# Sum transfers issued ahead of the weight sums, and down-projection weights loaded in single blocks

## The reference

```python
up = jnp.einsum('btd,df->btf', x, w_up)                 # 1024 -> 2 * 2816
hp = jnp.concatenate([conv_prefix, up], axis=1)
hc = conv_b + sum(conv_w[i] * hp[:, i:i + T] for i in range(CONV_WIDTH))   # width 3, per channel
g, u = hc[..., :D_FF], hc[..., D_FF:]
y = jnp.einsum('btf,fd->btd', jax.nn.gelu(g, approximate=False) * u, w_down)
x = layer_norm(DEEPNORM_ALPHA * x + y, ln2_g, ln2_b)
```

## Time and profile before

| What | Value |
| --- | --- |
| median of 3 runs | 2557.95 us (2546.45 to 2564.44) |
| the profiled execution | 2561.84 us, of which span 2560.1 us |
| PE busy | 2222.9 us (87%), 13868 matmuls |
| DVE, ACT, POOL busy | 63%, 41%, 36% |
| SP's DMA queue (q1) | 261.69 MB, 32.7% of the 16 DMA engines' span |
| POOL's DMA queue (q0) | 74.98 MB, 17.7% |

### The profile page before, as it was taken

The page is one execution under the profiler, slowest core; times in us unless marked ns, Lnnn a source line. Parts: engine busy times, 40 slices in busy tenths (PEclk is TensorE's granted clock), DMA queues, the critical chain, the costliest instruction groups (busy, mean ns, idle before and its releaser), DMA issues.

```text
span 2560.1 us, 35253 instructions
## 1 busy us (share of the span) xinstructions
PE 2222.9 (87%) x13868; PEld 1989.6 (78%) x13868; DVE 1609.4 (63%) x2064; ACT 1044.0 (41%) x1867; POOL 930.9 (36%) x554
## 2 busy tenths in 40 slices
PE   7999998888788887599899999989889888876996
PEld 7987678888788885478788866789888887854875
DVE  1569668666665665355836686777566665662557
ACT  3227565333333334245522375553333333341543
POOL 1134255454444542301221334555444444332112
PEclk9999999999899998799999999999989999987998
DMA  6221462444444448969651215614434444599695
GB/s 167 67 52 36 126 187 77 113 106 105 106 111 104 103 102 261 273 168 221 165 153 43 56 32 161 195 63 112 106 94 119 103 116 100 127 274 263 160 212 155
DMA packets 257468, 338.92 MB, mean 132 GB/s; under 512 B 39184, under 2 KB 157712, under 8 KB 257232
## 3 DMA queue, kind: packets, MB, share of 16 engines
q1 hardware_dynamic: 222424, 261.69, 32.7%
q0 software_dynamic: 34880, 74.98, 17.7%
HBM read 217.65 MB, written 98.03 MB: 123 GB/s over the span
## 4 chain that ended last, share of the span: by engine, by line
PE 31%; DVE 17%; POOL 16%; DMA 16%; issue 10%; ACT 8%; SPq 1%; ACTq 0%; POOLq 0%; DVEq 0%
DMA e_scr<-hg 11%; PE ps L2718 10%; PE ps L2306 8%; DMA araw<-a_scr 5%; POOL wblk L973 4%; POOL wblk L969 3%; PE ps L2565 3%; POOL bl L961 3%; DVE hg L1878 2%; DVE hg L1875 2%; POOL wblk L980 2%; POOL wblk L977 2%; ACT hg L1311 2%; PE ps L2626 2%; ACT bh L1274 1%
## 5 line engine op out<-in xcount | busy, mean ns | idle before, releaser
L2626 PE MATMUL ps<-bt,bh 128*128 128x272 f32 (+1 forms) x3520 | 629.7, 303 | 152.4 <-ACT gu L1283 137.2
L2626 PEld LDWEIGHTS ps<-bt,bh 128*128 128x128 f32 x3520 | 535.6, 202 | 162.3 <-ACT gu L1283 145.9
L2626 PE MATMUL ps<-bt,bl 128*128 128x272 f32 (+1 forms) x1760 | 384.4, 300 | 0.0
L1274 ACT ACTIVATE bh<-wblk 128x512 fp32r<-128x512 f32 x308 | 181.5, 622 | 490.5 <-POOL wblk L973 283.9
L2718 PE MATMUL ps<-dh,ah 128*128 128x512 f32 x616 | 257.9, 419 | 100.7 <-DVE al L1918 98.4
L961 POOL TENSOR_TENSOR bl<-wblk,bh 128x512 fp32r<-128x512 f32 x98 | 160.3, 1638 | 427.4 <-ACT bh L1274 427.4
L2626 PEld LDWEIGHTS ps<-bt,bl 128*128 128x128 f32 x1760 | 295.2, 201 | 0.0
L2718 PE MATMUL ps<-dl,ah 128*128 128x512 f32 x616 | 252.0, 409 | 0.0
L2718 PE MATMUL ps<-dh,al 128*128 128x512 f32 x616 | 251.3, 408 | 0.0
L2626 PE MATMUL ps<-ba,bh 128*128 128x272 f32 (+2 forms) x1408 | 235.6, 289 | 16.3 <-DVE gu L1864 14.6
L1841 DVE TENSOR_TENSOR bl<-wblk,bh 128x512 fp32r<-128x512 f32 x210 | 165.0, 819 | 124.0 <-ACT bh L1274 124.0
(11 more groups left out here) (260 smaller groups left out, 4444.4 us busy)
## 6 DMA issues: line engine op xcount, KB each, us to landing
wblk<-in_w_up SPq DMA_DIRECT2D x88, 512.0 KB, 5.3
a_scr<-hg SPq DMA_DIRECT2D x44, 552.0 KB, 3.2
e_scr<-hg POOLq DMA_DIRECT2D x44, 512.0 KB, 7.0
araw<-a_scr SPq DMA_DIRECT2D x66, 256.0 KB, 8.4
araw<-e_scr SPq DMA_DIRECT2D x66, 256.0 KB, 6.1
w<-in_w_down POOLq DMA_DIRECT2D x16, 1024.0 KB, 16.6
wrow<-in_w_out SPq DMA_DIRECT2D x48, 256.0 KB, 5.1
wrow<-in_w_out SPq DMA_DIRECT2D x24, 512.0 KB, 4.5
```

The lines of the kernel that those rows point to most:

```text
L1274: act.activation(bh[b][:], block_of(f, b), ACT.Copy).then_inc(S["u_hi"], 1)
L2626: e = nc.tensor.matmul(up_half(f, b, n), lhs, rhs[:, c:HW_] if n else rhs[:, 0:c], start=(k == 0 and m == 0), stop=(k == HK - 1 and m == 2))
```

## The change

In the up loop POOL issues `act_add(k, 0)` and `act_add(k, 1)` behind the low half of B_12 and ahead of the four weight sums, instead of after them; `act_add(k, 2)` stands before B_S3's sum instead of after it.

In the down stage w21, w22 and w12 are loaded in 33 transfers of 256 KB, one per step of SP's list from s = 4 to s = 36, in order of use, on two semaphores; block `i` waits for block `i - 2` to have landed. The rows for the residual come back one per step (s = 5 to 8 and s = 20 to 23). POOL's first weight sum moves behind R_TOP, and ACT's negated copies move by up to four steps. SP's wait for `adds1` moves from s = 14 to s = 20, and the second pair of gains from s = 26 to s = 38.

```diff
+            def down_block(l, i):
+                n, k = divmod(i, KP)
+                tile, c = ((w21, 0), (w22, HT), (w12, HT))[n]
+                if i >= 2:
+                    sp.wait_ge(S[f"wb{i % 2}"], wb_count(l, i - 2))
+                src = w_down[l].rearrange("(k two p) n -> two p k n", two=2, p=P)[1]
+                sp.dma_start(tile[:, k, :], src[:, k, c:c + HT]).then_inc(S[f"wb{i % 2}"], 16)
...
-                    elif s in (5, 7):
+                    elif 5 <= s < 9:
+                        if s == 6:
+                            sample_raw(l, 2)
                         z_back(l, s - 5)
-                        z_back(l, s - 4)
-                    elif s == 6:
-                        sample_raw(l, 2)
-                        down_block(l, "w21", 0, 0, 6)
-                    elif s == 8:
-                        down_block(l, "w21", 1, 6, KP)
...
-                    elif s == 12:
-                        down_block(l, "w12", 2, 8, KP)
-                    elif s in (14, 16):
-                        if s == 14:
-                            sp.wait_ge(S["adds1"], 16 * KP * (l + 1))
-                        z_back(l, s // 2 - 3 + (s - 14) // 2)
-                        z_back(l, s // 2 - 2 + (s - 14) // 2)
-                    elif s == 15:
-                        sp.wait_ge(S["sm_lo"], 4 * (l + 1))
-                        down_block(l, "w12", 0, 0, 4)
-                    elif s == 17:
-                        down_block(l, "w22", 0, 0, KP)
...
+                    elif 20 <= s < 24:
+                        if s == 20:
+                            sp.wait_ge(S["adds1"], 16 * KP * (l + 1))
+                        z_back(l, s - 16)
+                    elif s == 26:
+                        sp.wait_ge(S["sm_lo"], 4 * (l + 1))
                         sp.wait_ge(S["neg"], neg_t(l, T_1, 0) + 1)
-                        down_block(l, "w12", 1, 4, 8)
-                    elif s == 26:
+                    elif s == 38:
...
+                    if s < 4 + 3 * KP:
+                        down_block(l, s - 4)
                     act_block(l, s)
...
                     lo_up(l, f, B_12)
+                    if f >= 3:
+                        act_add(l, (f - 3) // 2, 1 - f % 2)
                     for b in SUMS[:3]:
                         sum_up(l, f, b)
-                    sum_up(l, f, B_S3)
                     if f >= 5 and f % 2:
                         act_add(l, (f - 5) // 2, 2)
-                    if f >= 3 and f % 2:
-                        act_add(l, (f - 3) // 2, 0)
-                    elif f >= 4:
-                        act_add(l, (f - 4) // 2, 1)
+                    sum_up(l, f, B_S3)
...
-                weight_add(l, T_1, 0)
                 for t in range(4):
                     residual(l, t)
                 act_add(l, KP - 1, 1)
                 residual_add(l, R_TOP)
+                weight_add(l, T_1, 0)
+                act_add(l, KP - 1, 2)
+                residual_add(l, R_P1)
                 weight_add(l, T_1, 1)
-                act_add(l, KP - 1, 2)
                 weight_add(l, T_1, 2)
-                residual_add(l, R_P1)
```

More of the change, by code:

```diff
@@ L462, in zb_count, with wb_count @@
             return 16 * (4 * l + 4) if t == NB else 16 * (2 * l + 2 + len(range(t // 2, NTOK, XS)))
+        def wb_count(l, i):
+            return 16 * (l * len(range(i % 2, 3 * KP, 2)) + i // 2 + 1)
         def rows_bank(i):
@@ L623, in up_cols, with first_blocks @@
                         .then_inc(S[f"wu_landed{f % 2}"], 16)
[L625 to L630, removed]
+            def first_blocks(l, n, k0, k1):
+                src = w_down[l].rearrange("(k two p) n -> two p k n", two=2, p=P)[0][:, k0:k1, 0:HT]
+                at_ = w12[:, 4 + k0:4 + k1, :] if k0 < 4 else w11[:, k0:k1, :]
+                sp.dma_start(at_, src).then_inc(S[f"wc_landed{n}"], 16)
+            def down_block(l, i):
[5 more added lines that the diff above has]
+                sp.dma_start(tile[:, k, :], src[:, k, c:c + HT]).then_inc(S[f"wb{i % 2}"], 16)
             def act_block(l, s):
@@ L848, in body @@
                         sp.wait_ge(S["u_lov"], lo_n(l, FT - 2, B_S4))
-                        down_block(l, "w11", 0, 0, 2)
-                        down_block(l, "w11", 1, 2, 4)
+                        first_blocks(l, 0, 0, 2)
+                        first_blocks(l, 1, 2, 4)
                         sample_raw(l, 0)
@@ L861, in body @@
                 sp.wait_ge(S["u_p"], 7 * (l + 1) * FT)
-                down_block(l, "w11", 2, 4, 7)
-                down_block(l, "w11", 3, 7, KP)
+                first_blocks(l, 2, 4, 7)
+                first_blocks(l, 3, 7, KP)
                 for s in range(4, NST):
@@ L881, in body @@
                         neg_out(l, KP - 1, 1)
-                    elif s == 12:
-                        down_block(l, "w12", 2, 8, KP)
-                    elif s in (14, 16):
-                        if s == 14:
-                            sp.wait_ge(S["adds1"], 16 * KP * (l + 1))
-                        z_back(l, s // 2 - 3 + (s - 14) // 2)
-                        z_back(l, s // 2 - 2 + (s - 14) // 2)
-                    elif s == 15:
-                        sp.wait_ge(S["sm_lo"], 4 * (l + 1))
-                        down_block(l, "w12", 0, 0, 4)
-                    elif s == 17:
-                        down_block(l, "w22", 0, 0, KP)
                     elif s == 18:
                         conv_rows(l, NRB - 1)
-                    elif s == 21:
+                    elif 20 <= s < 24:
[4 more added lines that the diff above has]
+                        sp.wait_ge(S["sm_lo"], 4 * (l + 1))
                         sp.wait_ge(S["neg"], neg_t(l, T_1, 0) + 1)
-                        down_block(l, "w12", 1, 4, 8)
-                    elif s == 26:
+                    elif s == 38:
                         sp.wait_ge(S["e_out"], 16 * KP * (l + 1))
@@ L1336, in weight_neg @@
                 elif which == T_3:
-                    act.wait_ge(S["w12"], 48 * (l + 1))
+                    for i in (2 * KP + k1 - 1, 2 * KP + k1 - 2):
+                        act.wait_ge(S[f"wb{i % 2}"], wb_count(l, i))
                     out, src = w12, w12[:, k0:k1, :]
@@ L1354, in down_hi @@
                     act.wait_ge(S[f"wc_landed{slot}"], wc_count(l, OUTU + slot))
[L1355 to L1358, removed]
+                elif p in (P_2, P_3):
+                    i = k + (KP if p == P_3 else 0)
+                    act.wait_ge(S[f"wb{i % 2}"], wb_count(l, i))
                 else:
@@ L1594, in body @@
                         scaled_gains(l)
-                        weight_neg(l, T_1, 0)
                     elif s == 6:
@@ L1599, in body @@
                         sample_hi(l, 3)
-                        weight_neg(l, T_1, 1)
+                        weight_neg(l, T_1, 0)
                     elif s == 10:
                         first_out(l)
-                    elif s == 11:
-                        weight_neg(l, T_1, 2)
+                    elif s in (12, 15):
+                        weight_neg(l, T_1, s // 3 - 3)
                     elif s in (26, 30, 33):
                         weight_neg(l, T_2, (26, 30, 33).index(s))
[L1607 to L1610, removed]
+                    elif s in (36, 38, 40):
+                        weight_neg(l, T_3, s // 2 - 18)
+                    elif s in (41, 42, 44):
+                        weight_neg(l, T_4, (41, 42, 44).index(s))
                     elif 58 <= s < 63:
```

## The result

The changed kernel takes **2332.09 us** (median of 4 runs, 2325.63 to 2335.54) against 2557.91 us for the kernel before on the same chip: a ratio of **0.9119**, 95% interval 0.908 to 0.9157. The forecast was 2342 us.

What follows compares the result with a forecast made beforehand. Bound: in the up stage a late landing of POOL's adding transfer, in P_1 and P_2 the DMA engines. 2561.8 (profiled) - 182 - 34 = 2346, which stands 3.9 above the median, so 2342 us; range 2290 to 2420.

Steps and rivals of the forecast that it cites:

- what bounds the kernel now: Up stage: PE held by ACT's tap_gate, which waits for POOL's adding transfer to land; P_1 and P_2: DMA engines.
- Rival E: Up stage: the landing was not the last to come, tap_gate has another reason to wait; no chance of its own.
- Step 1: Up loop, adds ahead of the sums: turn 26.4 to 21.6 us, issue priced 0.1 to 0.4; 91 us a layer, 182 in both.
- Rival A: Up loop: the issue can't start beside DVE's tap and is paid in full, 22.6 us a turn, 2380 us; chance 0.14.
- rival D: Up loop: the add's wait for e_out, ahead of the sums, makes it slower than before, 2632 us; chance 0.04.
- rival C: Up loop: the add's landing in its new place takes 16 instead of 7.0 to 9.83 us, 2426 us; chance 0.05.
- Step 2: Down stage, weights in single blocks: P_1 and P_2 win 23 us, P_3 loses 6; net 17 a layer, 34 in both.
- rival B: Down stage gives nothing, as SP waits for blocks, and P_3 pays: +8 us a layer, 2392 us; chance 0.14.
- w12, 2.9 MB, 9 us: Down stage: w12's load leaves the stretch before s = 22, taking 9 us of DMA time with it.
- term for R_BOT and its rows: Down stage: R_BOT, 12.6 us, and about half of the rows fetched at s = 20 to 23, 3 us, leave P_1 and P_2.
- Not won: the four scalings: Down stage: rz_top's four scalings stay back to back; they hold DVE's split of a tile for 11.87 us.
- Step 3: Down stage, the rest: SP's issues of 33 blocks are hidden and later landings have slack; cost 0.

Runs made afterwards that it cites:

- e1: The kernel before with only the up loop's new order, the adds ahead of the sums; down stage as before: 2356.20 us, ratio 0.9211.
- e3: The changed kernel with one further 64 KB transfer issued by POOL right behind the add in each turn: 2347.19 us, ratio 0.9177.
- e4: The changed kernel with three further 64 KB transfers issued by POOL right behind the add in each turn: 2388.82 us, ratio 0.9335.
- e9: The changed kernel with act_add(k, 0) and act_add(k, 1) moved from ahead of to behind the first three weight sums: 2368.57 us, ratio 0.9273.
- e2: The changed kernel with the up loop's order put back, so only the down stage's part of the change: 2530.67 us, ratio 0.9888.
- e6: The changed kernel with four semaphores for blocks, so SP waits for block i - 4 instead of i - 2: 2329.79 us, ratio 0.9119.
- e10: The changed kernel with the bias adds R_TOP and R_BOT cut to 64 of 1024 columns: 2309.73 us, ratio 0.9046.
- e11: The changed kernel with w12 loaded in three transfers at s = 12, 15 and 21, as before the change: 2329.68 us, ratio 0.9124.
- e8: The changed kernel with the last four residual rows and the adds1 wait back at s = 14 and 16: 2344.24 us, ratio 0.9174.
- e7: The changed kernel with six large weight transfers in the same order instead of single blocks, no wait for blocks: 2335.29 us, ratio 0.9135.
- e5: The changed kernel with POOL waiting, ahead of each residual scaling, for its own scaling before: 2329.68 us, ratio 0.9112.

## Why the prediction was right

**The bound (step "what bounds the kernel now")** was read rightly: the landing that led the chain was the last thing that `tap_gate` waited for, and it is gone. Rival E falls with that.

**Step 1, the adds ahead of the sums: right in mechanism, 17 us too small.** 91 us a layer were forecast; it was 101.3 and 97.7 by `tap_gate`, 202 us in both by e1. The term that was mis-sized is the price of the issue, "0.1 to 0.4" us a turn: it is 0, and the turn is 21.2 us, PE's own, instead of 21.6. The working had it nearly right: "an issue of 1.1 us in that place costs nothing". The row of 1.20 us is what POOL is held for, B_S1's sum ends 0.16 us later for it, and B_S2's not at all; it was the 0.4 of a longer issue, added on top, that cost 15 us of the forecast. Where the working was too easy is that B_S2's sum is safe "in any case": a late sum of B_S1 holds DVE's product, and by e3 and e4 that is paid in full from 1.35 us on. Rival A needed the issue to wait for the end of DVE's tap; it ran beside it, 726.91 to 728.11 against a tap until 728.13, and B_S2's sum ends at 12.68, not over 13. The Trainium skill (SBUF — State Buffer, "SBUF: two separate sides") says of two-port modes only that descriptors can't be written beside DVE, and no such wait shows beside this instruction.

**The wait for `e_out` (rival D)** cost nothing: the issue has no wait in front of it. **The landing (rival C)** became shorter, 5.8 us in place of 7.0; e9 shows that this hangs on the place, and that a late landing would have cost what C says in kind.

**Step 2, the down stage: right sum, two wrong terms.** P_1 and P_2 won 20.1 and 17.3 us (forecast 23), P_3 lost 1.8 and 2.6 (forecast 6), net 33.0 in the profiles against 34; by e1 and e2 it is 24 to 29 us of the runs' time. That SP's wait was harmless (rival B) is shown by e6, and that the DMA engines bound the stretch by e10, where 2.0 MB less make it 8.9 us shorter. But "w12, 2.9 MB, 9 us" failed: e11 puts 2.4 MB of it back, for 5.0 us of the engines' time, and loses 2.6 us there, none in the total. Time per MB from a whole-span share is not what a further MB costs in a full stretch. Of the term for R_BOT and its rows, 12.6 + 3 us, e8 has 11.4 us of engine time for R_BOT, near its 12.6; the rows never left the stretch, so their 3 us are 0, and 3.1 us of other transfers of SP took part of R_BOT's room. What is left is 8.4 us (110.40 against 102.05), of which P_3 gives 1.8 back, and 6 us a layer in total. That the sum came out near is luck in part, errors that cancel: too much for w12 and the rows, too much for P_3. So it is with the whole: step 1 was 17 to 20 us too small, step 2 5 to 10 us too large, and 2342 met 2332. Of the 24 to 29 us of this part e8 accounts for 12, e6, e7 and e11 for none; the other 12 to 17 belong to what was never undone alone (the first four rows one per step, POOL's first weight sum behind R_TOP, R_P1 ahead of the next two, w21's order), and stay open.

"Not won: the four scalings" held: the split still took 11.14 us. **Step 3, the rest at 0,** is not contradicted: e7 bears out that the 33 issues cost nothing.

## What to carry to other kernels

When a chain leads from a transfer's landing to an engine's next turn, look for the earliest place in the issuing engine's list at which the data is ready, and pay for the issue there only what it moves of the end of the work behind it; here that work was itself held up by another engine, which gave 1.35 us of free room, for an issue of 1.20, and no more. Take the length of the issue's own row for what it holds, not the distance to the start of the next row. In a stretch with full DMA engines, find out what can leave it, and price it by undoing, not by the mean time of a MB. A wait of the issuing queue or a long instruction there may be only where the shortage of the DMA engines shows: taking it away (e5, e6) gave nothing that the runs can tell.

## What the runs showed of the hardware

- An issue on POOL holds the work behind it until the end of its row, 1.20 us for a 512 KB adding transfer and 1.04 for a plain one of 64 KB, though the next row begins 0.77 and 0.60 us after its start: a sum of 1.29 us ends 1.31 to 1.33 us after the last issue's row (changed kernel, e3, e4). The issue itself runs beside a DVE tap (1.20 us, 726.91 to 728.11, against 725.85 to 728.13).
- Whether POOL or DVE waits for the other is settled by whose row starts first: a sum 0.1 us ahead of the product stretched the product from 1.30 to 2.90 us (e4); 1.2 us ahead, to 1.76 (e3). Four scalings back to back held DVE's split of 0.68 us for 11.14 us; with a semaphore wait between them, for 4.30 (e5).
- The same 512 KB adding transfer lands in 5.9 us when it is issued 7.7 us after `tap_gate` and in 8.3 us when it is issued at 14.0 (medians of nine, e9). Which neighbour slows it wasn't tried.
- A further plain MB in a stretch with a DMA share of 1.00 cost 1.1 us (e11), a MB of bias adds 4.4 us (e10), where the whole-span shares had given 3.2 and 6.0.
